# A gated delta rule whose zero-padded 128-wide matmuls become 64x64 array tiles

## The chip, the core and the metric

The kernel runs on one core of one Trainium2 chip. The metric is the device time of one execution in microseconds (us), the median of several runs. The profile is one further execution, recorded by the hardware profiler; its span is the time from the first to the last instruction.

## What is computed

A layer of two blocks over 1024 tokens of width 1024, all in float32. The first block is an attention layer (grouped heads and a neighbourhood attention), the second joins a gated delta rule (4 heads of size 128) with a dilated attention (8 heads of size 64). The change lies in the gated delta rule alone. The reference cuts the sequence into 16 chunks of 64 tokens and computes, per head:

```
a_mat = where(tril_strict, (k*beta) @ k.T * decay, 0)
l_mat = a_mat + eye(64)
u = solve(l_mat, v * beta)                  # X @ (v * beta)
w = solve(l_mat, k * beta * exp(gc))        # X @ (k * beta * exp(gc))
attn_intra = (q @ k.T) * decay
step over the chunks:
    v_new = u_i - w_i @ state
    o_i = (q_i * exp(gc)) @ state + attn_i @ v_new
    state = state * exp(gc_last) + k_tail_i.T @ v_new
```

## The kernel before, in words

The whole layer is one program with hand-written instruction streams for five engines, joined by semaphores. After the projections of the second block comes the delta stage (`delta_part`, L1773), about 157 us of the span, and after it the dilated attention (`causal_part`, L2458).

The delta stage works on tiles of 128 tokens, which are two chunks of 64: partitions 0 to 63 hold chunk 0 and 64 to 127 chunk 1. There are N = 8 tiles. `order` (L1835) writes the order of one iteration out by hand, the same for every engine, and the engines run it for i = 0 to 9. In iteration i three things are in flight:

- `front` on tile i: transposes and scales keys and values (`keys`, `values`, `khat_turn`, plain 128x128 TensorE transposes), the Gram matrix (`gram`, L1962) and the in-chunk attention (`attn`, L1972), and the masks. GpSimd (POOL) forms `kbe` and `ktail` in `khat_turn` (L2356, L2359) and six masked copies of the matrix A, `mask_levels` (L2385).
- `inv` on tile i-1: the inverse X of the triangular matrix, in LEVELS - 1 = 5 levels. Each is a product `z` (L1987), a copy by ScalarE (L2273), a product `update` (L2002) and a subtraction on VectorE (L2152) followed by a 32x32-block transpose (L2154) except at the last level. Here the zs and updates are already 64x64 matmuls, one for each head and chunk.
- `apply_u`, `apply_w` and `rec` on tile i-2: u = X (v beta) (L2011), w = X (k beta exp gc) (L2020), the two recurrence steps, each a `read` (L2038: w and q against the state S) and a `write` (L2051: the state's increment), and `attend` (L2058: in-chunk attention times v_new), and the sum of the output (`finish`, L2193).

u, w and `attend` are 128x128 matmuls, one per head, over both chunks at once. So that the chunks don't mix, their left operands are zero off the diagonal blocks: X is written at its last level by two half-height subtractions (L2149) into the padded `Xf`, and `attnT` by two half-height products (L2132) into a padded tile. Both are zeroed once by GpSimd in the first iteration (L2361, L2362). The write has a chunk's 64 rows and all 128 columns of `ktail` as weights. Every float32 matmul is recorded in the trace as two passes, each with a weight load of its own, so 4 heads make 8 passes.

The operations of one iteration are named here as z1 to z5, upd1 to upd5, read0, write0, read1, write1. TensorE's order in a full iteration is: z1, u, upd1, w, keys, z2, read0, upd2, khat, values, z3, write0, upd3, gram, z4, read1, upd4, attn, z5, write1, upd5, attend.

ScalarE's order around the change is: copy of Z (L2273), the exponential into `wq` (L2278), the copy of u (L2289), the decays (L2220 to L2230, seven small instructions), the copy of w (L2297), the copy of Z at level 2. Read0 waits for the copy of w.

Of the kernel before, what the change touches and what calls it, by code (L numbers as in the profile page):

```python
# [21 lines left out]
ALU = mybir.AluOpType  # L22
# [1750 lines left out]
def delta_part(nc, g, k, ps, gates, projection):  # L1773
# [13 lines left out]
    attnT = k.sb("d_attnT", [P, 3, H4, P])  # L1787
    T = k.sb("d_T", [P, 2, H4, CHUNK])
    X = k.sb("d_X", [P, 2, H4, CHUNK])
    Xf = k.sb("d_Xf", [P, 2, H4, P])  # L1790
# [30 lines left out]
    def blocks(a):  # L1821
# [8 lines left out]
             "S_zeroed zeroed o_summed").split()  # L1830
# [84 lines left out]
    def tensor(pe, following):  # L1915
# [60 lines left out]
        class inv:  # L1976
# [28 lines left out]
            @staticmethod  # L2005
            def apply_u(t):
                pe.wait_ge(s["X_ready"], (LEVELS - 1) * (t + 1))
                pe.wait_ge(s["vb_ready"], t + 1)
                pe.wait_ge(s["khatT_ready"], min(t + 2, N))
                for h in range(H4):  # L2010
                    last = nc.tensor.matmul(bank(1)[:, h, :], Xf[:, t % 2, h, :], vb[:, t % 2, h, :], start=True, stop=True)  # L2011
                last.then_inc(s["uw_ready"], 1)

            @staticmethod
            def apply_w(t):
# [3 lines left out]
                for h in range(H4):  # L2019
                    last = nc.tensor.matmul(bank(5)[:, h, :], kbe[:, t % 2, h, :], Xf[:, t % 2, h, :], start=True, stop=True)  # L2020
                last.then_inc(s["uw_ready"], 1)

        class rec:
# [19 lines left out]
            def write(t, c):  # L2043
# [4 lines left out]
                if n < 2 * N - 1:  # L2048
                    pe.wait_ge(s["attnT_ready" if c == 0 else "A_ready"], min(t + 2 + c, N))
                    for h in range(H4):  # L2050
                        last = nc.tensor.matmul(bank(2 * c)[:, h, :], ktail[r, t % 3, h, :], vnew[r, h, :], start=True, stop=True)  # L2051
# [3 lines left out]
            def attend(t):  # L2055
                pe.wait_ge(s["w_copied"], t + 1)
                for h in range(H4):
                    last = nc.tensor.matmul(bank(5)[:, h, :], attnT[:, t % 3, h, :], vnew[:, h, :], start=True, stop=True)  # L2058
# [11 lines left out]
    def vector(dve, following):  # L2070
        class front:
# [47 lines left out]
            def attn(t):  # L2119
                dve.wait_ge(s["level_masked"], LEVELS * t + 1)  # L2120
                nc.vector.tensor_tensor(T[:, t % 2, :, :], levels[:, LEVELS + 1, :].unsqueeze(1).to_broadcast([P, H4, CHUNK]),
                                        Al[:, t % 2, 0, :, :], ALU.subtract).then_inc(s["T0_ready"], 1)
                dve.wait_ge(s["T0_ready"], t + 1)
# [5 lines left out]
                dve.wait_ge(s["zeroed"], 1)  # L2129
                for c in range(2):  # L2130
                    r = chunk_rows(c)
                    last = nc.vector.tensor_tensor(attnT[r, t % 3, :, chunk_rows(1 - c)], own(0)[r], dec[r, 1, :, :], ALU.mult)  # L2132
                last.then_inc(s["attnT_ready"], 1)

        class inv:
# [5 lines left out]
            def update(t, l):  # L2141
                m = (LEVELS - 1) * t + l - 1
                dve.wait_ge(s["dX_ready"], m + 1)
                if l == LEVELS - 1:
                    if t >= 2:
                        dve.wait_ge(s["uw_ready"], 2 * (t - 1))
                    for c in range(2):
                        r = chunk_rows(c)
                        last = nc.vector.tensor_tensor(Xf[r, t % 2, :, r], X[r, t % 2, :, :], own(4)[r], ALU.subtract)  # L2149
                    last.then_inc(s["X_ready"], 1)  # L2150
                else:
                    nc.vector.tensor_tensor(X[:, t % 2, :, :], X[:, t % 2, :, :], own(4), ALU.subtract).then_inc(s["X_ready"], 1)  # L2152
# [54 lines left out]
    def scalar(act, following):  # L2207
# [58 lines left out]
        class inv:  # L2266
# [25 lines left out]
            def apply_w(t):  # L2292
# [4 lines left out]
                nc.scalar.copy(w_cols, halves(bank(5))).then_inc(s["w_copied"], 1)  # L2297
# [27 lines left out]
    def gpsimd(pool, following):  # L2325
# [6 lines left out]
        class front:  # L2332
# [17 lines left out]
            def khat_turn(t):  # L2350
                pool.wait_ge(s["decays_done"], 2 * t + 1)
                nc.gpsimd.tensor_tensor(dec[:, 0, :, :], dec[:, 0, :, :], per_row(beta[:, t, :], CHUNK), ALU.mult).then_inc(s["dec_masked"], 1)
                pool.wait_ge(s["khat_ready"], t + 1)
                if t >= 2:
                    pool.wait_ge(s["uw_ready"], 2 * (t - 1))
                nc.gpsimd.tensor_tensor(kbe[:, t % 2, :, :], khat[:, :, :], per_row(be[:, t, :]), ALU.mult).then_inc(s["kbe_ready"], 1)  # L2356
                if t >= 3:
                    pool.wait_ge(s["dS_ready"], 2 * (t - 2))
                nc.gpsimd.tensor_tensor(ktail[:, t % 3, :, :], khat[:, :, :], per_row(etl[:, t % 3, 0:H4]), ALU.mult).then_inc(s["ktail_ready"], 1)  # L2359
                if t == 0:  # L2360
                    nc.gpsimd.memset(Xf[:, :, :, :], 0.0)  # L2361
                    nc.gpsimd.memset(attnT[:, :, :, :], 0.0).then_inc(s["zeroed"], 1)  # L2362
# [14 lines left out]
            def attn(t):  # L2377
# [3 lines left out]
                mask_levels(t, 2, LEVELS)  # L2381

# [837 lines left out]
```

## Time and profile before

| | us |
|---|---|
| runs (3): median, lowest, highest | 1566.07, 1561.85, 1566.69 |
| the profiled execution's own time | 1566.08 |
| its span | 1564.3 |
| mean granted TensorE clock in it | 0.982 of full speed |
| TensorE busy | 1495.9 |
| delta stage, within the span | 1174 to 1331 |

The profile's page lists the busy time of each engine: PE is TensorE's matmuls, PEld its weight loads, DVE is VectorE, ACT ScalarE, POOL GpSimd. A line of the timeline has the start, the duration from the first to the last of the instructions merged into it, the engine, the line of the kernel, the operation, the tiles out<-in, for TensorE the rows*columns of the array that the weights use and partitions x moving columns, and the count. In brackets stands how long the engine was idle before it and what ended that. The distance between the starts of two groups on PEld is what the first one costs; the durations include a latency that overlaps the next group.

### The profile page before, as it was taken

Reading aid. Unit: us, or ns where it says so; the run is one execution under the profiler, and the core shown is the slowest. Engines: PE = TensorE matmul, PEld = TensorE weight load, DVE = VectorE, ACT = ScalarE, POOL = GpSimd, SP = SyncE. Lnnn points to the kernel's source line nnn. Section 1 sums busy time; section 2 is a strip of 40 time slices with the busy share of each in tenths; the row PEclk is TensorE's granted clock in tenths of the full one; section 3 lists DMA queues with packets and bytes.
Section 4 is the critical chain, followed back from the end, with each engine's and each line's share of the span. In section 5 each row is a group of like instructions: output and inputs, shape, how many; then the busy total and the mean of one; then the engine's idle time right before and its main releaser. Section 6 shows DMA issues by size and latency. Waiting matters only on the chain.

```text
span 1564.3 us, 30384 instructions
## 1 busy us (share of the span) xinstructions
PE 1495.9 (96%) x12386; PEld 1304.0 (83%) x12386; DVE 818.1 (52%) x1511; ACT 628.4 (40%) x1297; POOL 413.6 (26%) x509
## 2 busy tenths in 40 slices
PE   6999999969999889998999999999997998899998
PEld 6999789958878667776799999888896887788887
DVE  5239510068888667744430705362514775888531
ACT  5322011147777467643332212332334443777300
POOL 0212221110000066623202212221206675334430
PEclk9999999989999999999999999999996999999999
DMA  8213102200000032266402335423120011211332
GB/s 251 52 52 108 54 32 73 75 12 1 1 1 1 1 109 59 66 128 188 149 14 37 57 81 89 67 55 53 28 78 26 22 36 56 95 57 59 121 122 81
DMA packets 84465, 103.50 MB, mean 66 GB/s; under 512 B 25375, under 2 KB 68543, under 8 KB 84328
## 3 DMA queue, kind: packets, MB, share of 16 engines
q1 hardware_dynamic: 84328, 101.56, 24.9%
q8 instruction: 100, 1.64, 0.4%
q14 instruction: 37, 0.30, 0.1%
HBM read 78.40 MB, written 23.12 MB: 65 GB/s over the span
## 4 chain that ended last, share of the span: by engine, by line
PE 52%; DVE 2%; ACT 2%; DMA 2%; issue 1%; POOL 1%; SPq 0%; ACTq 0%; DVEq 0%; POOLq 0%
PE s_ps L362 22%; PE s_ps L1174 9%; PE s_ps L2624 2%; PE s_ps L2610 2%; PE s_ps L2002 2%; PE s_ps L1987 2%; PE s_ps L2599 1%; DMA qT<-s_gate 1%; PE s_ps L2038 1%; PE s_ps L992 1%; PE s_ps L2051 1%; PE s_ps L973 1%; PE s_ps L2587 1%; PE s_ps L2600 1%; PE s_ps L1553 1%
## 5 line engine op out<-in xcount | busy, mean ns | idle before, releaser
L328 POOL TENSOR_TENSOR p_w_lo<-p_w_raw,p_w_hi 128x2048 fp32r<-128x2048 f32 (+1 forms) x27 | 127.1, 4707 | 541.2 <-ACT p_w_hi L312 541.2
L362 PE MATMUL s_ps<-p_w_hi,w_out_hi 128*128 128x256 f32 (+1 forms) x640 | 182.0, 284 | 0.1
L362 PE MATMUL s_ps<-p_w_hi,w_out_lo 128*128 128x256 f32 (+1 forms) x640 | 179.7, 281 | 0.0
L362 PE MATMUL s_ps<-p_w_lo,w_out_hi 128*128 128x256 f32 (+1 forms) x640 | 179.5, 281 | 0.0
L362 PE MATMUL p_ps<-p_w_hi,hT_hi 128*128 128x256 f32 x576 | 163.5, 284 | 3.0 <-DVE p_w_lo L322 3.0
L362 PE MATMUL p_ps<-p_w_lo,hT_hi 128*128 128x256 f32 x576 | 162.7, 282 | 0.0
L362 PE MATMUL p_ps<-p_w_hi,hT_lo 128*128 128x256 f32 x576 | 162.6, 282 | 0.0
L362 PEld LDWEIGHTS s_ps<-p_w_hi,w_out_hi 128*128 128x128 f32 x640 | 120.5, 188 | 1.0 <-issue 0.6
L362 PEld LDWEIGHTS s_ps<-p_w_lo,w_out_hi 128*128 128x128 f32 x640 | 120.8, 189 | 0.0
L362 PEld LDWEIGHTS s_ps<-p_w_hi,w_out_lo 128*128 128x128 f32 x640 | 120.6, 188 | 0.0
L312 ACT CAST p_w_hi<-p_w_raw 128x2048 fp32r<-128x2048 f32 (+1 forms) x28 | 53.5, 1909 | 160.2 <-DMA p_w_raw<-w_in 81.7
L362 PEld LDWEIGHTS p_ps<-p_w_hi,hT_hi 128*128 128x128 f32 x576 | 109.1, 189 | 3.4 <-issue 3.3
L362 PEld LDWEIGHTS p_ps<-p_w_lo,hT_hi 128*128 128x128 f32 x576 | 109.2, 190 | 0.0
L362 PEld LDWEIGHTS p_ps<-p_w_hi,hT_lo 128*128 128x128 f32 x576 | 109.0, 189 | 0.0
L799 DVE TENSOR_TENSOR a_pt_lo<-a_ps,a_pt_hi 128x512 fp32r<-128x512 f32 x128 | 82.3, 685 | 24.1 <-ACT a_pt_hi L859 24.1
L859 ACT CAST a_pt_hi<-a_ps 128x512 fp32r<-128x512 f32 x128 | 69.0, 590 | 55.1 <-PE a_ps L723 55.0
L794 DVE TENSOR_REDUCE a_stat<-a_ps 128x1 f32<-128x1024 f32 x64 | 77.8, 1215 | 2.2 <-PE a_ps L713 2.2
L362 PE MATMUL s_ps<-w_out_hi,p_w_hi 128*128 128x512 f32 x192 | 76.2, 397 | 0.0
L362 PE MATMUL s_ps<-w_out_hi,p_w_lo 128*128 128x512 f32 x192 | 75.7, 394 | 0.0
L362 PE MATMUL s_ps<-w_out_lo,p_w_hi 128*128 128x512 f32 x192 | 75.5, 393 | 0.0
L723 PEld LDWEIGHTS a_ps<-ident,tok 128*128 128x128 f32 x512 | 57.7, 142 | 21.3 <-ACT tok L851 17.3
L723 PE MATMUL a_ps<-ident,tok 128*128 128x128 f32 x512 | 69.0, 278 | 6.3 <-ACT tok L851 5.0
(299 smaller groups left out, 3658.3 us busy)
## 6 DMA issues: line engine op xcount, KB each, us to landing
p_w_raw<-w_in SPq DMA_DIRECT2D x27, 1024.0 KB, 8.5
s_gate<-p_spill SPq DMA_DIRECT2D x48, 128.0 KB, 1.8
kbT<-x SPq DMA_DIRECT2D x8, 512.0 KB, 6.4
b_w_raw<-w_out SPq DMA_DIRECT2D x8, 512.0 KB, 5.2
qT<-s_gate SPq DMA_DIRECT2D x8, 512.0 KB, 6.1
qT<-x SPq DMA_DIRECT2D x8, 512.0 KB, 3.2
s_x<-qT SPq DMA_DIRECT2D x8, 512.0 KB, 4.5
c_table<-s_line SPq DMA_DIRECT2D x8, 512.0 KB, 3.7
```

Of the source, the lines that this page charges most:

```text
L312: self.nc.scalar.copy(self.w_hi[:, c % 2, :, 0:w], self.raw[:, :, 0:w]).then_inc(self.w_hi_ready, 1)
L328: ops.tensor_tensor(self.w_lo[:, c % 2, :, 0:w], self.raw[:, :, 0:w], self.w_hi[:, c % 2, :, 0:w].bitcast(F32), ALU.subtract).then_inc(sel ...
L362: last = self.nc.tensor.matmul(out, lhs, rhs, start=(kt == 0 and i == 0), stop=(kt == KT - 1 and i == 2))
L723: last = nc.tensor.transpose(ps[:, 4 + half, j * P:(j + 1) * P], prob(u)[:, c // 2, (c % 2) * P:(c % 2) * P + P], g.ident[:, :])
L794: nc.vector.tensor_reduce(stat[:, 0, u:u + 1], s, AX.X, ALU.max, negate=True).then_inc(max_ready, 1)
L799: nc.vector.tensor_tensor(part(pt_lo, grp, half, i), ps[:, 4 + half, :].rearrange("p (c q) -> p c q", c=4), part(pt_hi, grp, half, i).bitc ...
L859: nc.scalar.copy(part(pt_hi, grp, half, i), ps[:, 4 + half, :].rearrange("p (c q) -> p c q", c=4)).then_inc(pt_hi_ready, 1)
L1174: last = self.nc.tensor.matmul(self.ps[:, 4 + n % 4, :], a, b[:, kt, cols], start=(kt == 0 and i == 0), stop=(kt == KT - 1 and i == 2))
L1987: last = nc.tensor.matmul(own(3)[r, h, :], Al[r, t % 2, l, h, :], X[r, t % 2, h, :], start=True, stop=True)
L2002: last = nc.tensor.matmul(own(4)[r, h, :], T[r, t % 2, h, :], Z[r, h, :], start=True, stop=True)
L2610: last = nc.tensor.transpose(ps[:, 4 + n % 2, (j - first) * P:(j - first + 1) * P], prob[:, u % 3, j * P:(j + 1) * P], g.ident[:, :])
L2624: last = nc.tensor.matmul(ps[q * HD:(q + 1) * HD, 6 + u % 2, 0:HD], prob_t[:, u % 3, j * P + q * HD:j * P + (q + 1) * HD], v[:, j, h * HD: ...
```

## The change

All products that kept the chunks apart by zeros are done as 64x64 array tiles, on the compact X and a compact attnT.

- u: for each head and chunk one matmul with X of the chunk (64x64) as weights and 128 columns moving: 16 passes in place of 8.
- w: for each head four 64x64 matmuls, one for each half of the key dimension and each chunk, 64 columns moving: 32 passes in place of 8. Chunk 0 goes to bank 5, chunk 1 to bank 7; ScalarE's copy gathers both.
- write: ktail's 128 columns as two halves of 64, 128 columns moving: 16 passes in place of 8.
- attend: one matmul for each head and chunk, 64x64 weights, 128 columns moving: 16 passes in place of 8.
- The last level writes X in place in one full-height subtraction, and attnT is written by one full-height product. Xf, the memsets and their semaphore go; `d_room` and `d_room2` keep the addresses of the other tiles.
- The wait that kept Xf from being overwritten before u and w of two tiles back moves to X's first write (`X0`).
- GpSimd's products `kbe` and `ktail` are put into a function `tails`; in iteration 0 it is called after the masks, in all later ones where they were.

```diff
-    attnT = k.sb("d_attnT", [P, 3, H4, P])
+    attnT = k.sb("d_attnT", [P, 3, H4, CHUNK])
...
-                    last = nc.tensor.matmul(bank(1)[:, h, :], Xf[:, t % 2, h, :], vb[:, t % 2, h, :], start=True, stop=True)
+                    for c in range(2):
+                        r = chunk_rows(c)
+                        last = nc.tensor.matmul(bank(1)[r, h, :], X[r, t % 2, h, :], vb[r, t % 2, h, :], start=True, stop=True)
...
-                    last = nc.tensor.matmul(bank(5)[:, h, :], kbe[:, t % 2, h, :], Xf[:, t % 2, h, :], start=True, stop=True)
+                    for d in range(2):
+                        for c in range(2):
+                            r = chunk_rows(c)
+                            last = nc.tensor.matmul(own(5 + 2 * c)[chunk_rows(c ^ d), h, :], kbe[r, t % 2, h, chunk_rows(c ^ d)],
+                                                    X[r, t % 2, h, :], start=True, stop=True)
...
-                        last = nc.tensor.matmul(bank(2 * c)[:, h, :], ktail[r, t % 3, h, :], vnew[r, h, :], start=True, stop=True)
+                        for d in range(2):
+                            dk = slice(d * HD, (d + 1) * HD)
+                            last = nc.tensor.matmul(bank(2 * c)[dk, h, :], ktail[r, t % 3, h, dk], vnew[r, h, :], start=True, stop=True)
...
-                    last = nc.tensor.matmul(bank(5)[:, h, :], attnT[:, t % 3, h, :], vnew[:, h, :], start=True, stop=True)
+                    for c in range(2):
+                        r = chunk_rows(c)
+                        last = nc.tensor.matmul(bank(5)[chunk_rows(1 - c), h, :], attnT[r, t % 3, h, :], vnew[r, h, :], start=True, stop=True)
...
+                if t >= 2:
+                    dve.wait_ge(s["uw_ready"], 2 * (t - 1))
                 dve.wait_ge(s["T0_ready"], t + 1)
                 nc.vector.transpose(blocks(X[:, t % 2]), blocks(T[:, t % 2])).then_inc(s["X0_ready"], 1)
...
-                dve.wait_ge(s["zeroed"], 1)
-                for c in range(2):
-                    r = chunk_rows(c)
-                    last = nc.vector.tensor_tensor(attnT[r, t % 3, :, chunk_rows(1 - c)], own(0)[r], dec[r, 1, :, :], ALU.mult)
-                last.then_inc(s["attnT_ready"], 1)
+                nc.vector.tensor_tensor(attnT[:, t % 3, :, :], own(0), dec[:, 1, :, :], ALU.mult).then_inc(s["attnT_ready"], 1)
...
-                if l == LEVELS - 1:
-                    if t >= 2:
-                        dve.wait_ge(s["uw_ready"], 2 * (t - 1))
-                    for c in range(2):
-                        r = chunk_rows(c)
-                        last = nc.vector.tensor_tensor(Xf[r, t % 2, :, r], X[r, t % 2, :, :], own(4)[r], ALU.subtract)
-                    last.then_inc(s["X_ready"], 1)
-                else:
-                    nc.vector.tensor_tensor(X[:, t % 2, :, :], X[:, t % 2, :, :], own(4), ALU.subtract).then_inc(s["X_ready"], 1)
+                nc.vector.tensor_tensor(X[:, t % 2, :, :], X[:, t % 2, :, :], own(4), ALU.subtract).then_inc(s["X_ready"], 1)
+                if l < LEVELS - 1:
...
-                nc.scalar.copy(w_cols, halves(bank(5))).then_inc(s["w_copied"], 1)
+                nc.scalar.copy(w_cols, ps[:, 5:8:2, 0:H4 * CHUNK].rearrange("p c (h j) -> p h c j", h=H4)).then_inc(s["w_copied"], 1)
...
-                if t == 0:
-                    nc.gpsimd.memset(Xf[:, :, :, :], 0.0)
-                    nc.gpsimd.memset(attnT[:, :, :, :], 0.0).then_inc(s["zeroed"], 1)
+                if t >= 1:
+                    tails(t)
...
                 mask_levels(t, 2, LEVELS)
+                if t == 0:
+                    tails(t)
```

## Rows read from the trace of the kernel before

**Rows 1.** The page: busy time and share of the span of each engine.

```profile
PE 1495.9 (96%) x12386; PEld 1304.0 (83%) x12386; DVE 818.1 (52%) x1511; ACT 628.4 (40%) x1297; POOL 413.6 (26%) x509
```

**Rows 2.** Busy time by stretch; after POOL: granted clock, DMA share, GB/s.

```profile
1180.00:1204.00 24.00, 17.05 (x221) 14.55 (x222) 10.76 (x23) 6.20 (x21) 17.18 (x22) 0.50 0.07 18
...
1206.00:1208.00 2.00, 2.00 (x31) 1.76 (x28) 1.01 (x3) 1.97 (x9) 0.01 (x1) 1.00 0.61 150
...
1250.00:1266.00 16.00, 15.88 (x248) 13.97 (x246) 11.94 (x24) 7.61 (x23) 11.18 (x14) 1.00 0.10 28
```

**Rows 3.** Timeline, weight loads of one iteration: start, duration, line, shape, count, idle.

```profile
1237.20 0.55 PEld L1987 LDWEIGHTS s_ps<-d_X,d_Al 64*64 64x64 f32 x16
1237.81 0.97 PEld L2011 LDWEIGHTS s_ps<-d_vb,d_Xf 128*128 128x128 f32 x8
1238.90 0.55 PEld L2002 LDWEIGHTS s_ps<-d_Z,d_T 64*64 64x64 f32 x16
1239.51 0.97 PEld L2020 LDWEIGHTS s_ps<-d_Xf,d_kbe 128*128 128x128 f32 x8
1240.40 0.47 PEld L1925 LDWEIGHTS s_ps<-ident,kT 128*128 128x128 f32 x4
...
1241.78 0.97 PEld L2038 LDWEIGHTS s_ps<-d_S,d_wq 128*128 128x128 f32 x8 [0.20 <-ACT d_wq L2297]
...
1244.50 0.54 PEld L1987 LDWEIGHTS s_ps<-d_X,d_Al 64*64 64x64 f32 x16 [0.17 <-issue]
...
1247.43 0.57 PEld L1987 LDWEIGHTS s_ps<-d_X,d_Al 64*64 64x64 f32 x16
...
1250.48 0.57 PEld L1987 LDWEIGHTS s_ps<-d_X,d_Al 64*64 64x64 f32 x16 [0.17 <-issue]
1251.12 0.96 PEld L2051 LDWEIGHTS s_ps<-d_vnew,d_ktail 64*128 64x128 f32 x8
...
1252.81 0.97 PEld L2058 LDWEIGHTS s_ps<-d_vnew,d_attnT 128*128 128x128 f32 x8
...
1253.90 0.55 PEld L1987 LDWEIGHTS s_ps<-d_X,d_Al 64*64 64x64 f32 x16
```

**Rows 4.** Timeline, weight loads of a float32 product with 384 moving columns.

```profile
863.72 0.09 PEld L1258 LDWEIGHTS s_ps<-conv_y,bl_rel 33*8 33x8 f32 x1 [0.24 <-issue]
864.04 0.09 PEld L1258 LDWEIGHTS s_ps<-conv_y,bl_rel 33*8 33x8 f32 x1 [0.23 <-issue]
```

**Rows 5.** Timeline, ScalarE and VectorE in the iteration of rows 3.

```profile
1239.07 0.59 ACT L2289 COPY d_u<-s_ps 128x512 f32<-128x512 f32 x1 [0.23 <-PE s_ps L2011]
...
1245.22 0.98 DVE L2077 TENSOR_TENSOR d_tl<-d_gch,d_gc 128x4 f32<-128x4 f32 x1
...
1246.31 0.69 DVE L2182 TENSOR_TENSOR d_S<-d_Sg,s_ps 128x512 f32<-128x512 f32 x1
...
1246.93 0.42 DVE L2152 TENSOR_TENSOR d_X<-d_X,s_ps 128x256 f32<-128x256 f32 x1
```

**Rows 6.** Timeline, the first iteration: A, the memsets, the masks and z1.

```profile
1178.86 0.42 DVE L2116 TENSOR_TENSOR d_A<-s_ps,d_dec 128x256 f32<-128x256 f32 x1 [1.26 <-PE s_ps L1962]
...
1180.94 1.38 POOL L2362 MEMSET d_attnT<- 128x1536 f32 x1
...
1182.28 1.40 POOL L2385 TENSOR_TENSOR d_Al<-d_A,d_levels 128x256 f32<-128x256 f32 x2
...
1184.49 0.93 PEld L1987 LDWEIGHTS s_ps<-d_X,d_Al 64*64 64x64 f32 x16 [5.01 <-DVE d_X L2124]
```

**Rows 7.** Timeline, weight loads of the last two iterations.

```profile
1304.00 0.54 PEld L1987 LDWEIGHTS s_ps<-d_X,d_Al 64*64 64x64 f32 x16
...
1308.20 0.97 PEld L2038 LDWEIGHTS s_ps<-d_S,d_wq 128*128 128x128 f32 x8 [0.26 <-ACT d_wq L2297]
...
1319.87 0.97 PEld L2011 LDWEIGHTS s_ps<-d_vb,d_Xf 128*128 128x128 f32 x8
...
1323.02 0.97 PEld L2038 LDWEIGHTS s_ps<-d_S,d_wq 128*128 128x128 f32 x8 [1.20 <-ACT d_wq L2297]
```

More of the change, by code:

```diff
@@ L1786, in delta_part @@
     ktail = k.sb("d_ktail", [P, 3, H4, P])
-    attnT = k.sb("d_attnT", [P, 3, H4, P])
+    attnT = k.sb("d_attnT", [P, 3, H4, CHUNK])
+    k.sb("d_room", [P, 3, H4, CHUNK])
     T = k.sb("d_T", [P, 2, H4, CHUNK])
     X = k.sb("d_X", [P, 2, H4, CHUNK])
-    Xf = k.sb("d_Xf", [P, 2, H4, P])
+    k.sb("d_room2", [P, 2, H4, P])
     u = k.sb("d_u", [P, 2, H4, P])
@@ L1829, in delta_part @@
              "u_copied w_copied wS_ready vnew_ready av_ready dS_ready S_ready Sg_ready oq_ready o_ready osq_ready "
-             "S_zeroed zeroed o_summed").split()
+             "S_zeroed o_summed").split()
     s = {n: k.sem("d_" + n) for n in names}
@@ L2352, in khat_turn @@
                 nc.gpsimd.tensor_tensor(dec[:, 0, :, :], dec[:, 0, :, :], per_row(beta[:, t, :], CHUNK), ALU.mult).then_inc(s["dec_masked"], 1)
[L2353 to L2359, printed above, removed]
-                if t == 0:
-                    nc.gpsimd.memset(Xf[:, :, :, :], 0.0)
-                    nc.gpsimd.memset(attnT[:, :, :, :], 0.0).then_inc(s["zeroed"], 1)
+                if t >= 1:
+                    tails(t)
             @staticmethod
@@ L2381, in attn, with tails @@
                 mask_levels(t, 2, LEVELS)
+                if t == 0:
+                    tails(t)
+        def tails(t):
+            pool.wait_ge(s["khat_ready"], t + 1)
+            if t >= 2:
+                pool.wait_ge(s["uw_ready"], 2 * (t - 1))
+            nc.gpsimd.tensor_tensor(kbe[:, t % 2, :, :], khat[:, :, :], per_row(be[:, t, :]), ALU.mult).then_inc(s["kbe_ready"], 1)
+            if t >= 3:
+                pool.wait_ge(s["dS_ready"], 2 * (t - 2))
+            nc.gpsimd.tensor_tensor(ktail[:, t % 3, :, :], khat[:, :, :], per_row(etl[:, t % 3, 0:H4]), ALU.mult).then_inc(s["ktail_ready"], 1)
         def mask_levels(t, first, end):
```

## The prediction

> **What bounds the kernel now.** The page gives TensorE 96% of the span [rows 1], which says little about one stage, so the next view is busy time by stretch. In the steady part of the delta stage TensorE is busy 15.88 of 16 us at full clock, VectorE 11.94, GpSimd 11.18, ScalarE 7.61; in the first iterations the clock is at half, 1.2 GHz, and it is back at 2.4 GHz by 1206 [rows 2]. Third, the timeline of TensorE's weight loads over one iteration: the distance of two starts is what a group costs [rows 3]. z1 returns after 1253.90 - 1237.20 = 16.70 us. TensorE sets the pace, yet not alone: read0 ends 0.20 us of idleness caused by ScalarE's copy of w [rows 3].
>
> What the groups cost shows where array time goes. w, followed by transposes of its own shape, costs 1240.40 - 1239.51 = 0.89 for 8 passes, 0.111 each. u, the same matmuls, but followed by a 64x64 group, costs 1238.90 - 1237.81 = 1.09: 0.20 more. z1, 16 passes of 64x64, costs 0.61 [rows 3]. A pass is bound by its moving columns: with 384 columns and only 8 weight columns the loads are 864.04 - 863.72 = 0.32 apart, 0.83 ns a column [rows 4], so 64 columns are 0.053 and 128 are 0.107. Sixteen passes of 64 in a row would be 0.85; z1 takes 0.61, so the two chunks' tiles run side by side. Eight pairs at 0.053 plus the 0.005 that w's 0.111 has over 0.107 are 0.47, and the remaining 0.14 is what the change of array shape costs here: about 0.05 for the first load, which nothing hides, and 0.09 at the end.
>
> **The change, part by part.** *Padding.* u: 16 passes of 128 columns, two tiles at a time, are 8 x 0.111 = 0.89, just as now; half the array did zeros, but a 64-wide tile streams its columns no faster. The write (two column tiles of the same rows) and attend are 0.89 too. So the halved arithmetic gives nothing, and in u and attend the number of instructions doubles.
>
> *w.* 32 passes of 64 columns. If pairs run as in z1: 16 x 0.058 = 0.93. If all four quarters of the array run at once: 0.47. No row has four tiles; I take the nearest, 0.93, and keep 0.47 as the other end. The Trainium skill, "TensorE: Matmul & The Clock Gate", section "Wait — 56ns, not 53.3ns?", says that matmuls never start closer than about 25 ns; by that w would be 32 x 0.025 = 0.80, an estimate, and the sum below about 0.3 us lower. z1's 0.47 over 16 passes is 29 ns, so no row here shows the floor.
>
> *Changes of shape.* This is what the change removes. In z3, write0, upd3 two of them go: 0.20 and 0.14, so 0.34. The stretch z5, write1, upd5, attend, z1, u, upd1, w becomes one run of 64x64 tiles. It costs now 1253.90 - 1250.48 = 3.42 and 1240.40 - 1237.20 = 3.20, together 6.62. After: 0.05 + four groups of 0.47 + three of 0.89 + 0.93 + 0.09 = 5.62. TensorE's own work falls by 1.00 + 0.34 = 1.34 us an iteration.
>
> *What gives part of it back.* (a) z1 to read0. ScalarE copies u at 1239.07, which is 1.26 after u's first load (0.89 plus 0.37 of latency), then does seven decay instructions and the copy of w; read0 starts 1241.78 - 1239.07 = 2.71 later [rows 3, 5]. After: 0.47 + 1.15 (u without its unhidden 0.11 load) + 2.71 = 4.33 in place of 4.58. TensorE would need 0.47 + 0.89 + 0.47 + 0.93 + 0.14 + keys 0.44 + z2 0.61 = 3.95, so ScalarE decides and 0.25 is saved. w's copy, still 512 columns, is late for no other reason. (b) z3 to z4, now 2.93: VectorE's small L2077 holds it until 1246.20, behind it come S (0.62 to the next start), then X3 (0.42) [rows 5], and z4 waits for X3. From z3 that is 1.70 + 0.62 + 0.42 + 0.08 = 2.82, whatever TensorE does: saved 0.10 of the 0.34. (c) z5 to z1 of the next iteration: 0.05 + 0.47 + 0.89 + 0.47 + 0.89 = 2.77 in place of 3.42, saved 0.65. It is free of others: S can start at 1.64 after z5, X5 follows at about 2.6 and is ready at 3.0, and u wants it at 2.77 + 0.47 = 3.24. Here VectorE's two half-height subtractions and two half-height products become single instructions, about 0.8 us less of its 12; as TensorE and ScalarE are ahead of it, I give it nothing beyond making that 3.0. read0 to z3 and z4 to z5 keep their shapes and times. Sum: 0.25 + 0.10 + 0.65 = 1.00 us, 15.70 an iteration. Bounds: 0.6 if (c) loses 0.4 to VectorE, 1.34 if nothing is given back; six full iterations: **-6.0** (3.6 to 8.0).
>
> *The added and moved waits.* X0 now waits for u and w of two tiles back. They ran at the head of the same iteration, some 12 us before: nothing. Behind it on VectorE stand only attnT, S and X5. w needs bank 7 free, which the wait for the last output already ensures.
>
> *GpSimd in iteration 0.* A is ready at 1178.86 + 0.42 = 1179.28, but GpSimd first does kbe, ktail and the memsets and starts the masks at 1182.28, and z1 waits 5.01 us [rows 6]. With the memsets gone and `tails` after the masks, mask 0 starts about 1179.35: 2.9 earlier, and z1 with it. kbe and ktail are then done about 1186.4, and the next khat waits for them 1 us; z2's update on TensorE is still running then, so that costs nothing. The bound below: the clock is at half from before here to after 1204 [rows 2]. Should it rise at the same moment as before, 2.9 us more of dense work run at half speed, +1.5. I take the middle, +0.7: **-2.2** (-1.4 to -3.0).
>
> *The last two iterations.* With `front` gone, w is on the path. From z1 to read0 it takes 4.20 now [rows 7], where z1 at 1304.00 also confirms the period: (1304.00 - 1253.90) / 3 = 16.70; after: 0.47 + 0.89 + 0.47, then w to its last pass 0.87, latency 0.37, copy 0.59, 0.04 = 3.70: -0.50. From u to read0 3.15 now [rows 7]; after 0.89 + 0.87 + 0.37 + 0.59 + 0.04 = 2.76: -0.39. Between them as (b) and (c): -0.75. Together **-1.6**, with w at 0.47 it is -2.5, and -1.0 if (c) fails.
>
> **The sum** is -6.0 - 2.2 - 1.6 = -9.8 us. The profiled execution took 1566.08 (span 1564.3), the median is 1566.07, so both give 1556.3. The attention behind it is unchanged and simply starts earlier. A measurement can tell about 0.3%, 4.7 us, from no change.
>
> **The rivals.**
> *More is kept* (0.10). Four tiles run at once and VectorE's lighter queue lets z4 go earlier: 6 x 1.34 + 3.0 + 2.5 = 13.5, 1552.5.
> *ScalarE and VectorE take it back* (0.14). VectorE's chain S, X5, output already runs without a gap around z1; if X5 comes late, u waits and its copy with it. Then 0.3 an iteration is left: 1.8 + 2.2 + 1.0 = 5 at most, and with the clock term at its worst 3.5: 1562.
> *The tiles take turns at 128 columns* (0.05). Pairs are shown for 64 moving columns only; the write with its one tile goes at 0.111. If a pair with 128 columns took turns, u, attend and both writes would be 16 x 0.111 = 1.78 each, 3.56 more, less 1.34: 2.2 us slower an iteration; six of them, half as much twice for the tail, less 2.2: +13, 1579. It decides against the change once a pair costs more than 0.111 + 1.34 / 32 = 0.153 us. Against it: z1's rate, and that weights of both tiles are separate.
> *One bank, two row tiles* (0.04). u and attend write both chunks' results into one bank, from different rows of the array. If such tiles exclude each other, u and attend cost 1.78 each: 1.78 more, less 1.34, +0.4 an iteration; with the start and end about 1566, no change. z1 does just this into one bank, in different partitions, and its tiles run side by side [rows 3]. The Trainium skill, "TensorEngine Tiling (Array Packing)", section "Gotcha 1: PSUM Pressure", says that different row tiles cannot access the same bank at once; z1's 0.61 disagrees where the partitions differ.
> *The clock falls in the long run of 64x64 tiles* (0.06). From 1180 to 1204 mostly 64-wide work ran with TensorE busy 17 of 24 us and the clock did not rise [rows 2]. If the 5.6 us run lost half its speed in each iteration: 6 x 5.6 = 34, less 10: 1590. It was, however, at half already when that work began and had gaps; the dense steady stretch holds full clock.
> That the change doesn't do what it says is no case of its own: shapes and operands stand in the code.
>
> **How the numbers follow.** The forecast has 0.61: 1556.3, its own range 1552 to 1560. The range of 8 in 10 takes in the larger gain and most of what is taken back: 1551 to 1562. Faster by over 0.3% means under 1561.4: 0.61 less 0.02, plus 0.10, plus 0.04 of the taken-back case: 0.73. Same: 0.02 + 0.10 + 0.04 = 0.16. Slower: 0.11.
>
> **What would show it.** Period of z1 15.7 us; z1 to u and upd1 to w 0.47; u, attend and write to the next group 0.89; w 0.93 or 0.47; ScalarE's copy of w ahead of read0 with more than 0.20 of idleness; z1 of the first iteration about 1181.5. I am wrong if the distance from u to upd1 stays at 1.09 or grows, if PEclk shows 0.50 after 1210, or if VectorE's X ends long waits ahead of u and z4.

## The result

| | before | after |
|---|---|---|
| runs: median (lowest to highest) | 1566.07 (1561.85 to 1566.69) | 1548.2 (1546.33 to 1549.99) |
| profiled execution: own time, span | 1566.08, 1564.3 | 1546.33, 1544.5 |
| mean granted clock in it | 0.982 | 0.990 |

A fourth execution of before, in the same comparison, puts its median at 1566.26. The ratio of the times is 0.9897, 95% interval 0.9884 to 0.9911: 14 to 18 us faster, where 9.8 were forecast. 1548.2 lies below the range of 1551 to 1562. The sign was right, the gain was too small.

The page of the kernel after has the engines' busy time, as [rows 1] has it for before:

```profile
PE 1470.3 (95%) x12826; PEld 1283.9 (83%) x12826; DVE 805.3 (52%) x1495; ACT 627.5 (41%) x1297; POOL 411.1 (27%) x507
```

TensorE has 440 more passes and is busy 25.6 us less; VectorE has 16 instructions fewer (two for each of the 8 tiles) and GpSimd two, the memsets. The same stretches as [rows 2]:

```profile
1180.00:1204.00 24.00, 19.97 (x355) 17.10 (x357) 12.15 (x27) 10.90 (x33) 19.42 (x24) 0.79 0.13 36
...
1250.00:1266.00 16.00, 15.05 (x336) 13.64 (x331) 12.12 (x24) 8.59 (x26) 12.54 (x15) 1.00 0.19 61
```

In the steady stretch TensorE, which had no idleness to speak of, now has nearly a microsecond of it in 16: something else has begun to decide. In the start of the stage the clock is 0.79 of full speed in place of 0.50, which the change does not explain by itself; more on that below.

The timeline of TensorE's weight loads over one iteration, to be laid beside [rows 3]:

```profile
1209.14 0.46 PEld L1988 LDWEIGHTS s_ps<-d_X,d_Al 64*64 64x64 f32 x12 [0.17 <-issue]
1209.46 0.13 PEld L2060 LDWEIGHTS s_ps<-d_vnew,d_ktail 64*64 64x64 f32 x1
...
1210.31 0.13 PEld L2003 LDWEIGHTS s_ps<-d_Z,d_T 64*64 64x64 f32 x1
...
1210.80 0.19 PEld L2069 LDWEIGHTS s_ps<-d_vnew,d_attnT 64*64 64x64 f32 x3
1210.86 0.14 PEld L2003 LDWEIGHTS s_ps<-d_Z,d_T 64*64 64x64 f32 x1
...
1210.97 0.47 PEld L2069 LDWEIGHTS s_ps<-d_vnew,d_attnT 64*64 64x64 f32 x8
1211.30 0.20 PEld L1988 LDWEIGHTS s_ps<-d_X,d_Al 64*64 64x64 f32 x4
1211.40 0.14 PEld L2069 LDWEIGHTS s_ps<-d_vnew,d_attnT 64*64 64x64 f32 x2
1211.41 0.20 PEld L1988 LDWEIGHTS s_ps<-d_X,d_Al 64*64 64x64 f32 x4
...
1212.11 0.85 PEld L2014 LDWEIGHTS s_ps<-d_vb,d_X 64*64 64x64 f32 x16 [0.27 <-DVE d_X L2153]
1212.93 0.60 PEld L2003 LDWEIGHTS s_ps<-d_Z,d_T 64*64 64x64 f32 x16
1213.40 0.60 PEld L2026 LDWEIGHTS s_ps<-d_X,d_kbe 64*64 64x64 f32 x32
1214.06 0.42 PEld L1926 LDWEIGHTS s_ps<-ident,kT 128*128 128x128 f32 x4
...
1215.97 0.97 PEld L2045 LDWEIGHTS s_ps<-d_S,d_wq 128*128 128x128 f32 x8 [0.77 <-ACT d_wq L2299]
```

Three things are to be seen. The groups no longer stand in a row: attend (L2069) begins while the last update (L2003) still runs, and z1 (L1988) runs between attend's passes; the write (L2060) starts 0.32 us after z5 (L1988), before z5's last passes. The 32 passes of w take 0.66 us up to the transposes, change of shape included. And two waits stand where there was 0.20 us in all: u waits 0.27 us for VectorE's X, read0 waits 0.77 us for ScalarE's copy of w (0.82 to 0.83 in the iterations behind it). The next u is at 1227.40; the five distances between u's groups from 1212.11 to 1288.79 are 15.29 once and then 15.34 to 15.35, where before had 16.64 and then 16.70 (1221.17 to 1304.61). In the text below this distance is the **period**, given as it is from the third u on: 16.70 before, 15.35 after.

VectorE ahead of that u has no idle time from its answer to read1 on; each instruction stands behind the one before it:

```profile
1207.92 0.69 DVE L2175 TENSOR_TENSOR d_vnew<-d_u,s_ps 64x512 f32<-64x512 f32 x1 [1.12 <-PE s_ps L2045]
...
1210.38 0.45 DVE L2137 STREAM_TRANSPOSE d_X<-d_T 128x256 f32<-128x256 f32 x1
1210.75 0.39 DVE L2142 TENSOR_TENSOR d_attnT<-s_ps,d_dec 128x256 f32<-128x256 f32 x1
1211.06 0.67 DVE L2184 TENSOR_TENSOR d_S<-d_Sg,s_ps 128x512 f32<-128x512 f32 x1
1211.65 0.41 DVE L2153 TENSOR_TENSOR d_X<-d_X,s_ps 128x256 f32<-128x256 f32 x1
```

Where the 19.8 us between the two spans lie, by the first weight loads of the same groups in both traces (the stage ends where the products of the dilated attention begin):

| stretch | before | after | difference | forecast |
|---|---|---|---|---|
| start to the first keys | 1173.77 | 1173.46 | -0.3 | 0 |
| first keys to first z1 (GpSimd's fill) | 10.72 | 7.54 | -3.2 | -2.9 |
| z1 to the second u (first iterations) | 36.68 | 31.11 | -5.6 | -1.0, and +0.7 for the clock |
| second to seventh u, five periods | 83.44 | 76.68 | -6.8 | -5.0 |
| seventh u to the end of the stage | 26.30 | 24.12 | -2.2 | -1.6 |
| dilated attention and the rest | 233.4 | 231.6 | -1.7 | 0 |

The fill is the sum's own step, seen here in the kernel after, against 5.01 us of idleness in [rows 6]:

```profile
1178.27 0.42 DVE L2127 TENSOR_TENSOR d_A<-s_ps,d_dec 128x256 f32<-128x256 f32 x1 [0.99 <-PE s_ps L1963]
1178.78 1.41 POOL L2390 TENSOR_TENSOR d_Al<-d_A,d_levels 128x256 f32<-128x256 f32 x2 [0.98 <-DVE d_A L2127]
...
1181.00 0.93 PEld L1988 LDWEIGHTS s_ps<-d_X,d_Al 64*64 64x64 f32 x16 [2.44 <-DVE d_X L2137]
...
1185.91 0.69 DVE L2098 TENSOR_TENSOR d_khat<-s_ps,l 128x512 f32<-128x512 f32 x1 [1.25 <-POOL d_ktail L2386]
```

The first mask starts 0.09 us after A is done (1178.27 + 0.42), where before it was 3.0, z1's idleness is halved, and the next khat does wait for ktail, 1.25 us, as forecast.

### The profile page after: what moved, and what is told of

It is laid out like the page before. It is cut to its first block, busy times and chain, and to the rows that moved or that the text cites. A ratio compares the mean times of both kernels' runs of the same rounds, so it can differ in the third digit from the quotient of the medians.

```text
span 1544.5 us, 31241 instructions
## 1 busy us (share of the span) xinstructions
PE 1470.3 (95%) x12826; PEld 1283.9 (83%) x12826; DVE 805.3 (52%) x1495; ACT 627.5 (41%) x1297; POOL 411.1 (27%) x507
## 4 chain that ended last, share of the span: by engine, by line
PE 49%; DVE 3%; DMA 3%; ACT 2%; issue 1%; POOL 1%; SPq 0%; DVEq 0%; ACTq 0%
PE s_ps L362 23%; PE s_ps L1174 9%; DMA qT<-s_gate 3%; PE s_ps L2629 2%; PE s_ps L2615 2%; PE s_ps L2604 1%; PE s_ps L2045 1%; PE s_ps L992 1%; PE s_ps L973 1%; PE s_ps L1988 1%; PE s_ps L2592 1%; PE s_ps L2003 1%; PE s_ps L2605 1%; PE s_ps L1553 1%; DVE conv_y L1749 1%
```

## The experiments

Twelve kernels ran in three groups, each group on one chip beside the kernel before (1565.13, 1563.92 and 1564.18 us there); the ratios are to these, and the changed kernel itself did not run again in them. Since a whole run moves by some 3 us with the clock that it was granted (the tile shapes alone took 1557.9 to 1559.1 us at a mean of 0.987 to 0.989, 1560.3 to 1564.2 at 0.983 to 0.985), the period in the trace is the sharper number: inside one execution the distances from the third u to the seventh agree within 0.03 us, but for three single ones that are named at their kernels. The first group takes the change apart.

**The tile shapes alone, in the kernel before.** X and attnT stay padded and are written by half-height instructions.

```diff
-                    last = nc.tensor.matmul(bank(1)[:, h, :], Xf[:, t % 2, h, :], vb[:, t % 2, h, :], start=True, stop=True)
+                    for c in range(2):
+                        r = chunk_rows(c)
+                        last = nc.tensor.matmul(bank(1)[r, h, :], Xf[r, t % 2, h, r], vb[r, t % 2, h, :], start=True, stop=True)
```

and likewise w, the write and attend.

> The kernel before with nothing changed but the shapes of u, w, write and attend: 64x64 tiles that read the diagonal blocks of the padded Xf and attnT. Memsets, GpSimd's order and VectorE's half-height instructions stay. Theory 1 (the array's own gain is larger than forecast, since four tiles run at once in w and neighbouring groups of 64x64 tiles overlap): z1 still starts near 1184.5 us, the period of u in the steady part is 15.4 to 15.7 us (16.70 before), and the time is 8 to 12 us under the kernel before. Theory 2 (the tiles give what was forecast, 1.0 us an iteration, and the rest of the gain is clock and start): period 15.7, time 6 to 8 us under the kernel before.

Measured: 1561.46 us (1557.94 to 1564.17), ratio 0.9975 [0.9965, 0.9986], some 4 us; period 16.26, only 0.44 under before. Both expectations named more. Timeline of this kernel around u, VectorE and TensorE's loads:

```profile
1253.19 0.82 DVE L2142 TENSOR_TENSOR d_attnT<-s_ps,d_dec 64x256 f32<-64x256 f32 x2
1254.04 0.69 DVE L2192 TENSOR_TENSOR d_S<-d_Sg,s_ps 128x512 f32<-128x512 f32 x1
1254.64 0.84 DVE L2159 TENSOR_TENSOR d_Xf<-d_X,s_ps 64x256 f32<-64x256 f32 x2
...
1255.54 0.85 PEld L2013 LDWEIGHTS s_ps<-d_vb,d_Xf 64*64 64x64 f32 x16 [1.17 <-DVE d_Xf L2159]
```

Each pair of half-height instructions takes 0.82 to 0.84 us, twice a full-height one, and u waits 1.17 us for the second. Group by group this trace has the distances of the kernel after to 0.05 us, except one: from z1 to u 1.72 us in place of 0.81. TensorE had done all that the new shapes let it do, and VectorE held back most of it: without the wait the period would be 16.27 - 1.17 = 15.10, an estimate. Of the 0.44 that came through, 0.22 lie between z3 and z4 (2.92 to 2.70), and 0.15 between z5 and u (4.04 to 3.89).

**The converse: the changed kernel with its two VectorE instructions halved.**

```diff
-                nc.vector.tensor_tensor(attnT[:, t % 3, :, :], own(0), dec[:, 1, :, :], ALU.mult).then_inc(s["attnT_ready"], 1)
+                for c in range(2):
+                    r = chunk_rows(c)
+                    last = nc.vector.tensor_tensor(attnT[r, t % 3, :, :], own(0)[r], dec[r, 1, :, :], ALU.mult)
+                last.then_inc(s["attnT_ready"], 1)
```

and the last subtraction from X in the same way.

> The kernel after with X's last level and attnT written by two half-height VectorE instructions each again (the tiles stay 64x64 and compact). Theory V (with the new tiles VectorE's queue ahead of u is the bound, so the 0.4 us that each pair of half-height instructions costs more is felt in full): u's period goes from 15.35 to 16.1 to 16.3 us, u waits about 1.1 us for X, the time is 5 to 7 us over the kernel after. Theory T (TensorE still sets the period and VectorE only fills its slack, as the prediction had it): 15.4 to 15.6 us, under 2 us in all.

Measured: 1556.32 us (1555.59 to 1557.72), ratio 0.9945 [0.9924, 0.9965], against 0.9897 for the changed kernel; period 16.33, so 0.98 us more.

```profile
1248.45 0.82 DVE L2144 TENSOR_TENSOR d_attnT<-s_ps,d_dec 64x256 f32<-64x256 f32 x2
...
1249.30 0.69 DVE L2193 TENSOR_TENSOR d_S<-d_Sg,s_ps 128x512 f32<-128x512 f32 x1
...
1249.90 0.84 DVE L2159 TENSOR_TENSOR d_X<-d_X,s_ps 64x256 f32<-64x256 f32 x2
...
1250.80 0.85 PEld L2014 LDWEIGHTS s_ps<-d_vb,d_X 64*64 64x64 f32 x16 [1.25 <-DVE d_X L2159]
```

The same rows as above, without any padding. Both ways the two instructions are worth 0.9 to 1.0 us an iteration, once the tiles are small.

**Only the subtraction halved.** The edit is the second half of the one before.

> The changed kernel, with the subtraction of the last product from X alone issued as two instructions of 64 partitions (0.84 us) instead of one of 128 (0.41); the masked attention stays one. Theory V (VectorE's chain of masked attention, state and X ahead of the u products is what binds there, so that each half adds its whole length): the distance between u's groups goes from 15.35 us to 15.35 + 0.4 = 15.8, half of what both splits gave (16.33), and the time is some 1552 us. Rival: only the masked attention binds, since it also holds back the state; then the distance stays within 0.15 us of 15.35, and the time near 1549.

Measured: 1552.72 us (1551.28 to 1553.69), ratio 0.9923 [0.9908, 0.9937]; period 15.78 (once 15.94), 0.43 over the changed kernel, and u waits 0.69 us. The two halves add, so what binds is a chain: masked attention, state, X, each behind the other on VectorE.

**The fill alone, in the kernel before.** kbe and ktail behind the masks in iteration 0, the memsets earlier in GpSimd's stream.

```diff
-                if t == 0:
-                    nc.gpsimd.memset(Xf[:, :, :, :], 0.0)
-                    nc.gpsimd.memset(attnT[:, :, :, :], 0.0).then_inc(s["zeroed"], 1)
+                if t >= 1:
+                    tails(t)
...
                 mask_levels(t, 2, LEVELS)
+                if t == 0:
+                    tails(t)
```

> The kernel before with only GpSimd's first iteration changed: kbe and ktail after the masks, and the two memsets run while GpSimd would wait for the first keys, 3 us earlier. Theory A (how long TensorE is idle before the first z1 decides how long the clock stays at half): z1 starts near 1181.5 us, the half-speed stretch is 10 to 17 us instead of 27, the time is 5 to 7 us under the kernel before. Theory B (the early return of the clock came from the denser tiles): the half-speed stretch stays at 24 us or more and the time is only 2 to 3 us lower.

Measured: 1560.92 us (1556.13 to 1562.74), ratio 0.9971 [0.996, 0.9982], some 4.5 us. First keys to z1 is 7.54 us, as in the changed kernel, and the period 16.70, as before. The half-speed stretch at the start of the stage is 10.2 us, as theory A had it. Its z1:

```profile
1183.17 0.93 PEld L1987 LDWEIGHTS s_ps<-d_X,d_Al 64*64 64x64 f32 x16 [2.44 <-DVE d_X L2124]
```

**The fill undone in the changed kernel.** kbe, ktail and memsets of two spare tiles of the old sizes stand ahead of the masks again.

> The kernel after, with kbe and ktail ahead of the masks again in the first iteration and 3.6 MB-free memsets of the two spare tiles (1.6 to 1.8 us in place of 2.3) behind them: nearly the start of before under the new tiles. Theory A: z1 starts near 1184, the half-speed stretch is back to 20 us or more, the time is 5 to 7 us over the kernel after (1553 to 1555). Theory B: the clock still returns after about 10 us, the time is 3 us over it (about 1551).

Measured: 1549.97 us (1548.05 to 1554.34), ratio 0.9911 [0.989, 0.9931]; first keys to z1 is 10.08 us, 2.5 longer, period 15.35. By the median 1.8 us, by the trace 2.5; the intervals overlap, so the trace carries this one. With the long wait back the half-speed stretch is still 10.2 us, so theory A, that this wait decides its length, does not hold.

**The write as one 64x128 product again.**

```diff
-                        for d in range(2):
-                            dk = slice(d * HD, (d + 1) * HD)
-                            last = nc.tensor.matmul(bank(2 * c)[dk, h, :], ktail[r, t % 3, h, dk], vnew[r, h, :], start=True, stop=True)
+                        last = nc.tensor.matmul(bank(2 * c)[:, h, :], ktail[r, t % 3, h, :], vnew[r, h, :], start=True, stop=True)
```

> The kernel after with the write as one matmul of 64x128 weights per head again, 8 passes. Theory 1 (changes of array shape are the cost): write0 to upd3 1.08 us as before and z3 to write0 0.61, so TensorE's work grows by 0.7 us an iteration; of it write1's part is felt (z5 to u grows by 0.3 to 0.5 us) and of write0's part at most 0.3, so 15.8 to 16.0 an iteration and 3 to 5 us over the kernel after. Theory 3 (VectorE's chain decides on both sides): under 0.2 us an iteration, the time within 1.5 us of the kernel after.

Measured: 1551.29 us (1549.45 to 1552.95), ratio 0.9915 [0.99, 0.993]; period 15.59, 0.24 more (once 16.49, in an iteration in which TensorE stood still 0.96 us ahead of read1 for nothing that the trace shows). Weight loads of this kernel from z5 on:

```profile
1213.02 0.57 PEld L1988 LDWEIGHTS s_ps<-d_X,d_Al 64*64 64x64 f32 x16 [0.17 <-issue]
1213.66 0.96 PEld L2058 LDWEIGHTS s_ps<-d_vnew,d_ktail 64*128 64x128 f32 x8
1214.74 0.43 PEld L2003 LDWEIGHTS s_ps<-d_Z,d_T 64*64 64x64 f32 x12
```

From z5 to the last update it is 1.72 us, where the changed kernel has 1.17: each write costs TensorE 0.5 us more, in changes of shape and in lost overlap. Only 0.24 in the iteration come through, 0.22 of it between z3 and z4; at z5 VectorE's chain decides anyway.

**Attend's results in its own chunk's partitions.** The sums of the other chunk's output then meet wrong partitions: this part of the output is not computed.

```diff
-                        last = nc.tensor.matmul(bank(5)[chunk_rows(1 - c), h, :], attnT[r, t % 3, h, :], vnew[r, h, :], start=True, stop=True)
+                        last = nc.tensor.matmul(bank(5)[r, h, :], attnT[r, t % 3, h, :], vnew[r, h, :], start=True, stop=True)
```

> The kernel after with attend's results at the rows of its own chunk, so that it uses the same two quarters of the array as z and upd and not the two others (the in-chunk part of the output is added to the wrong chunk). Theory O (attend ran at the same time as upd5 and z1, because it used the quarters that they leave free): attend's passes no longer mix with those of upd5 and z1, u comes 0.3 to 0.6 us later in each iteration, period 15.6 to 15.9, the time 2 to 4 us over the kernel after. Theory S (groups follow one another at the end of their columns whatever quarter they use): no change, 15.35.

Measured: 1550.44 us (1549.42 to 1551.71), ratio 0.9904 [0.988, 0.9928]; period 15.55, 0.20 more. Its loads around attend:

```profile
1230.35 0.19 PEld L2069 LDWEIGHTS s_ps<-d_vnew,d_attnT 64*64 64x64 f32 x2
...
1230.52 0.75 PEld L2069 LDWEIGHTS s_ps<-d_vnew,d_attnT 64*64 64x64 f32 x13
1231.17 0.13 PEld L1988 LDWEIGHTS s_ps<-d_X,d_Al 64*64 64x64 f32 x1
1231.24 0.13 PEld L2069 LDWEIGHTS s_ps<-d_vnew,d_attnT 64*64 64x64 f32 x1
1231.28 0.54 PEld L1988 LDWEIGHTS s_ps<-d_X,d_Al 64*64 64x64 f32 x13
```

z1 now starts when attend is at its last passes, 0.82 us after attend's first; in the changed kernel it started 0.50 us after it and ran between its passes. From z5 to z1 it is 2.48 us in place of 2.16. Of these 0.32 us 0.20 are felt, less than the 0.3 to 0.6 expected: u still starts 3.00 us after z5 (2.97), since VectorE decides there, but ScalarE copies the later z1 first and so comes to u's copy 1.35 us after u's start in place of 1.20. There attend uses the two quarters of the array that lead from a chunk's rows to the other chunk's columns, z and the updates the two others. The same tiles of the same sizes, moved into their neighbours' quarters, lose most of the overlap: it is one of quarters.

**w with the loop over halves outside** (d, h, c in place of h, d, c), so that passes for the same two quarters follow each other.

> The kernel after with w's loops in the order half of the key dimension, head, chunk, so that only two quarters of the array are in use at a time; same instructions. Theory F (four tiles run at once in w): w to the transposes goes from 0.67 to 1.1 us. In the steady part read0 waits 0.8 us for ScalarE, so the period stays 15.35; the last two iterations take 0.4 us more each and the time is within 1.5 us of the kernel after. Theory P (w was quick for another reason, such as the end of upd1 overlapping): w stays at 0.67.

Measured: 1549.9 us (1548.5 to 1551.97), ratio 0.9904 [0.9882, 0.9926]; period 15.34 to 15.35, unchanged.

```profile
1213.90 0.84 PEld L2026 LDWEIGHTS s_ps<-d_X,d_kbe 64*64 64x64 f32 x32
1214.82 0.42 PEld L1926 LDWEIGHTS s_ps<-ident,kT 128*128 128x128 f32 x4
...
1216.43 0.19 PEld L2045 LDWEIGHTS s_ps<-d_S,d_wq 128*128 128x128 f32 x1 [0.48 <-ACT d_wq L2299]
```

w takes 0.92 us to the transposes in place of 0.66, so the order in which the quarters are used costs 0.26, and read0 waits 0.48 in place of 0.77. What all four quarters at once saved had gone into that wait whole. Only the last distance between u's groups, where the next tile's decays are gone from ScalarE, shows it: 13.82 in place of 13.55.

**Work that holds the clock.** 36 transposes whose results nobody reads, 14 behind the values of the first tile and 22 ahead of the first z1.

> The kernel after with 36 transposes of the identity into an unused bank while TensorE would wait at the start of the stage: 14 ahead of the first gram, 22 ahead of the first z1. If idleness there is what lowers the clock, and its phase decides when it returns, the granted clock stays at 1.00 through 1174 to 1200, the first iteration shrinks from 15.1 to 12.5 to 13.5 us, the mean clock rises from 0.9875 to 0.992 or more, and the time is 2 to 4 us under the kernel after and varies less from run to run. If the clock falls anyway in the gaps of the first iteration, nothing is gained, or up to 1 us lost.

Measured: 1549.34 us (1544.68 to 1551.51), ratio 0.9895 [0.9868, 0.9923], no different from the changed kernel. The 2 to 4 us expected did not come. In its profiled execution the half-speed stretch at the start of the stage was 3.4 us in place of 10.2, and from z1 to u it took 14.98 us in place of 15.81; but keys came at 1178.13, 4.7 later, in a part of the program ahead of the transposes, whose wait this kernel also had tightened. The 0.8 us are shown; whether more is to be had stays open.

**VectorE's mask behind the subtraction.** The third group tries the two waits that the change created. The product that writes attnT, with its waits, goes from its old place in VectorE's order into a function that the end of the iteration calls, behind the last subtraction from X.

```diff
-                nc.vector.tensor_tensor(attnT[:, t % 3, :, :], own(0), dec[:, 1, :, :], ALU.mult).then_inc(s["attnT_ready"], 1)
...
+        if f and mask_attn:
+            mask_attn(i)
```

> The changed kernel, with VectorE's masking of the attention moved from ahead of the state to behind the last subtraction from X. It takes 0.39 us, of which the u products wait 0.27 for X. Theory V: the distance between u's groups falls by up to 0.27 us, to 15.1, and the time by some 2 us, to 1546. Rival: TensorE's own passes (write, last inverse product, attend) end so late that VectorE, started earlier, waits for them instead: within 0.05 us of 15.35, no difference in the time.

Measured: 1546.18 us (1545.32 to 1547.37), ratio 0.988 [0.9863, 0.9896]; period 15.08, 0.27 less, and u no longer waits. This is also what the tile shapes alone would have without their wait (15.10).

**ScalarE's copy of w first.** The exponentials of the decays (1.06 us for four stay; 0.42, 0.19 and 0.20 us move) go from ahead of the copy of w to behind the copy of z2.

```diff
-                act.wait_ge(s["dec_cut"], 2 * t + 1)
-                nc.scalar.activation(dec[:, 0, :, :], dec[:, 0, :, :], ACT.Exp, scale=-1.0)
...
+                if l == 2 and t + 1 < N:
+                    exponentials(t + 1)
```

> The changed kernel, with ScalarE's exponentials of the next decays (1.06, 0.42, 0.19 and 0.20 us) moved from ahead of the copy of w to behind the copy of the second inverse product. In the changed kernel the read of the state waits 0.77 to 0.83 us for the copy of w, although the w products ended 1.2 us before it began. Theory: what the four w tiles saved ends in this wait (splitting them into pairs again cost no time), so the distance between u's groups falls by 0.5 to 0.75 us, to 14.6 to 14.85, and the time to 1542 to 1545. Rival: the exponentials, now later, hold back the next copy of the inverse or VectorE's mask by as much: within 0.1 us of 15.35 or above.

Measured: 1546.48 us (1542.92 to 1548.32), ratio 0.9881 [0.9862, 0.9899]; period 14.70 as the rule (once 14.88), 0.65 less. ScalarE and TensorE's loads in this kernel:

```profile
1227.71 0.60 PEld L2026 LDWEIGHTS s_ps<-d_X,d_kbe 64*64 64x64 f32 x32
1228.10 1.06 ACT L2233 ACTIVATE d_dec<-d_gch,d_g 128x64 f32<-128x64 f32 x4
...
1229.07 0.57 ACT L2305 COPY d_wq<-s_ps 128x512 f32<-128x512 f32 x1
...
1229.68 0.97 PEld L2045 LDWEIGHTS s_ps<-d_S,d_wq 128*128 128x128 f32 x8 [0.18 <-ACT d_wq L2305]
...
1229.96 0.42 ACT L2212 ACTIVATE d_dec<-d_dec 128x256 f32<-128x256 f32 x1
```

The copy starts 1.36 us after w's first pass, where the same iteration of the changed kernel has 2.01, and the wait falls from 0.83 to 0.18; what is left ahead of the copy are the four decays of the next tile, 1.06 us.

**Both moves.**

> Both moves at once: VectorE's mask behind the subtraction from X, ScalarE's exponentials behind the copy of the second inverse product. If the two waits are one after the other on one chain, the gains add: up to 1.0 us an iteration, 1540 us. If one cover hides both, it is as the better of the two alone.

Measured: 1543.36 us (1541.15 to 1544.21), ratio 0.9861 [0.9847, 0.9876]; period 14.43, 0.92 under the changed kernel: the two gains add up in full. The interval of its ratio lies below that of the changed kernel (0.9884 to 0.9911); those of the two single moves overlap with it, so for them the period is the evidence. This version beats before and after.

## Why the prediction was wrong

**What the forecast missed, in numbers.** Between the two spans it missed 10.0 us (19.8 against 9.8). The clock is 5.9 of them: +0.7 was forecast, about -5.2 came. The period is 2.1 (six of 0.35), the stretch from z1 to the first u 0.8, the last two iterations 0.6, the fill 0.3 and the time ahead of the stage 0.3. So two terms failed: the clock's, which was luck and which is taken up below, and the change's own, the period.

**The period, forecast 15.70, measured 15.35.** The working had three parts, and they can be read off the same distances.

- (a) **z1 to read0, ScalarE decides: right in what decides.** From u to read0 the forecast has 4.33 - 0.47 = 3.86 us; measured are 1215.97 - 1212.11 = 3.86, and 3.91 in the iterations behind it (before: 3.97). w was indeed faster than ScalarE could use. The forecast named the reason, seven decay instructions ahead of the copy, and stopped there; moving three of them was worth more per iteration (0.65) than the tile shapes alone (0.44).
- (b) **z3 to z4: 2.82 forecast, 2.70 measured.** The state's update started 1.61 us after z3 (1220.30 - 1218.69) and not 1.70, since the write runs into z3's last passes and S no longer waits for it. 0.1 us.
- (c) **z5 to z1: the step that failed.** "2.77 in place of 3.42, saved 0.65. It is free of others". The 2.77 added five groups, each at its price alone. In the trace z1 starts 1211.30 - 1209.14 = 2.16 us after z5. The prediction had read from z1 that two tiles of one group run side by side, and from that derived 0.47 a group; it did not ask whether tiles of different groups do too. They do: the write starts 0.32 us behind z5, attend before the update ends, z1 between attend's passes. With attend in its neighbours' quarters TensorE needs 0.32 us more here, of which 0.20 is felt; with the write as a whole tile it needs 0.55 us more (1.72 in place of 1.17 up to the update), of which nothing is felt at this place.

And it was not free of others. From z5 to u the forecast was 2.77 + 0.47 = 3.24, set by TensorE, with X ready at 3.0. u started 1212.11 - 1209.14 = 2.97 after z5, when X was ready, and TensorE wanted it 0.27 earlier: VectorE had become the bound at this place. That X came on time was in part luck. S was to start 1.64 after z5, by the write; it started 1.92 after it (1211.06), held by the masked attention ahead of it on VectorE. VectorE's X ending a wait ahead of u was one of the prediction's own signs of being wrong. Hence the sentence "I give it nothing beyond making that 3.0" hid the size of the thing: with the instructions halved X comes 0.9 to 1.0 later, and then so does u. The prediction put the whole of (c) to the tile shapes. The runs put 0.44 of the 1.35 us to the shapes and 0.91 to the two merged VectorE instructions, given the shapes. What the merged instructions give without the new shapes was not tried: the padded layout needs two. The same instructions account for the 0.8 us from z1 to the first u, where the forecast had nothing: with the clock back late this takes 19.28 us in before, with the tile shapes alone and with both halved, 18.84 with X halved, and 18.43 with both merged.

**w: 0.93 taken, 0.47 kept as the other end.** The other end is the right one: 0.66 us to the transposes, of which 0.14 to 0.20 is the change of shape. In the full iterations it made no difference, as read0 waits for ScalarE. The estimate of 0.80 us for w by the floor of about 25 ns between matmuls (the Trainium skill, "TensorE: Matmul & The Clock Gate", section "Wait — 56ns, not 53.3ns?") is above what the trace shows: even with the change of shape counted in, 0.66 / 32 is 21 ns a pass.

**The fill: -2.9 forecast, -3.2 measured**, and 2.5 to 3.2 in the two kernels that isolate it. Right.

**The clock term had the wrong sign.** The forecast gave +0.7 for the clock's rise at a fixed moment. In the profiled execution of before, half speed lasted from 1178.1 for 27.3 us; in that of after from 1180.0 for 10.2. Of the thirteen traces other than that with the held clock seven have the clock back 8.6 to 9.8 us behind the first z1 (after, both fill kernels, whole write, w in pairs, w copy first, both moves) and six 20.9 to 21.4 (before, tile shapes alone, both VectorE halves, X halved, attend, mask later); among these are kernels whose instructions up to there are the same as in after, and which came back late (X halved, attend). So this is the execution's, not the change's; what tips it no run shows. What it is worth can be read off the changed kernel's relatives: z1 to u takes 15.6 to 15.8 us with the early rise and 18.4 with the late one, and the next distance of the mask-later kernel is 15.94 instead of 15.02. That is 3.5 us of the profiled difference, and the 1.7 us behind the stage goes with a stretch of 3.4 us at half speed at 1335 that before has and after has not: in the four traces with such a stretch (before, fill alone, w in pairs, held clock) what follows the stage takes 232.8 to 233.6 us, in the others 231.6 to 232.2. Without both, and without the 0.3 us ahead of the stage, the two spans differ by 14.3 us: 3.2 for the fill, 8.1 for six periods of 1.35, 2.2 at the end, and 0.8 from z1 to the first u. 14 lies at the lower end of what the medians allow (14 to 18). Taken from 1566.1 it gives 1551.8, an estimate that lies just inside the forecast's range: the change itself was forecast at 10.5, without the clock's +0.7, and gave 14.3.

**The rivals.** "More is kept" (13.5 us, 1552.5) is nearest: four tiles at once, and z4 earlier. Its mechanism holds only in part, since what w saved was lost again in the full iterations, and the larger share of the period came with the merged VectorE instructions. "ScalarE and VectorE take it back" named both waits that appeared, and overrated them; its 3.5 us with the clock term at its worst is a slip, by its own terms it is 1.8 + 1.4 + 1.0 = 4.2. Tiles that take turns at 128 columns, tiles that exclude each other in one bank, and a falling clock did not occur: u's 16 passes take 0.82 us, and the granted clock in [rows 2]'s steady stretch is 1.00 in both kernels. The rule of the Trainium skill, "TensorEngine Tiling (Array Packing)", section "Gotcha 1: PSUM Pressure", that different row tiles cannot access one bank at once, is not borne out where the partitions differ: u and attend write both chunks' results into one bank and keep the pace of pairs.

## What to carry to other kernels

When tiles shrink to a quarter of the array, cost the groups of a run together, not one by one: neighbours that use other quarters overlap, and the order of the loops inside a group decides how many quarters work at once. Then lay the new need of TensorE beside the chain of each engine that feeds it, at each border: here u, with the new shapes alone, waited 1.17 us for VectorE. A wait that appears after a change is the next thing to move: two reorderings on VectorE and ScalarE, without any new arithmetic, gave 0.92 us an iteration more, and added up.

## What the runs showed of the hardware

- Passes of neighbouring groups run between each other when they use other quarters of the array: attend and z1 alternate in runs of 2 to 4 passes, and z5 to z1 took 2.16 us, 2.48 with attend in its neighbours' quarters.
- w's 32 passes of 64 columns took 0.66 us with quarters alternating and 0.92 us with the pairs in sequence, for the same work.
- A VectorE product or subtraction over 64 partitions takes as long as over 128: two took 0.82 to 0.84 us, one full-height one 0.39 to 0.42.
- Kernels with the same instructions up to the first z1 got full speed back some 9 or some 21 us after it; 3.5 us of span hang on that, as much as some of the edits here gave.
